# A hybrid decoder step on one core: attention units with a lag of three, exponentials between copies, and cached pages in two groups

## What is computed

```
s = einsum('bhmqk', q, k) * ATTN_SCALE           # two maps m, causal mask
p = softmax(s)                                   # per map
attn = p[map 0] - lam * p[map 1]
o = attn @ v ; o = o * rsqrt(mean(o^2) + eps) * g * (1 - lam_init)
```

## Time and profile before

| what | value |
|---|---|
| median of three runs | 4176.69 us |
| the profiled execution, its own time | 4166.23 us |
| its span | 4164.5 us |
| mean granted TensorE clock | 0.896 |
| PE, DVE, ACT, POOL busy over the span | 84%, 46%, 32%, 38% |
| attention phase in the span (first load to the next phase's first load) | 2593.1 to 3205.8 us |
| first and last row maximum (units 0 and 63) | start at 2618.43 and 3181.89 us |
| row maximum of unit 28, of unit 43 | start at 2889.82 and 3011.80 us |

### The profile page before, as it was taken

The page is one execution under the profiler, slowest core; times in us unless marked ns, Lnnn a source line. Parts: engine busy times, 40 slices in busy tenths (PEclk is TensorE's granted clock), DMA queues, the critical chain, the costliest instruction groups (busy, mean ns, idle before and its releaser), DMA issues. The chain is left out here.

```text
span 4164.5 us, 78261 instructions
## 1 busy us (share of the span) xinstructions
PE 3483.6 (84%) x34038; PEld 3147.2 (76%) x34038; DVE 1899.8 (46%) x2159; ACT 1346.4 (32%) x2059; POOL 1563.1 (38%) x648
## 2 busy tenths in 40 slices
PE   5889686898897298999999999455775989999896
PEld 2888435888786188999999998333443889999896
DVE  3333606455542586353454430677433772522622
ACT  1111113433432134333333433333444333333332
POOL 0111000000000155656656665455000656556563
PEclk8999858999998599999999999667887999999998
DMA  5222123334331543445444665545353534444442
GB/s 191 83 85 73 46 92 126 122 113 149 114 105 48 167 124 115 133 131 152 141 138 140 183 188 158 193 152 202 137 202 102 163 104 139 127 138 140 125 141 71
DMA packets 710476, 546.83 MB, mean 131 GB/s; under 512 B 34763, under 2 KB 667491, under 8 KB 709885
## 3 DMA queue, kind: packets, MB, share of 16 engines
q1 hardware_dynamic: 664182, 473.18, 36.9%
q10 hardware_dynamic: 45606, 67.55, 4.7%
q0 software_dynamic: 352, 1.18, 0.1%
HBM read 471.55 MB, written 70.29 MB: 130 GB/s over the span
## 5 line engine op out<-in xcount | busy, mean ns | idle before, releaser
L1630 POOL TENSOR_TENSOR dense_w_lo<-dense_w_raw,dense_w_hi 128x1024 fp32r<-128x1024 f32 x504 | 1273.4, 2532 | 974.8 <-ACT dense_w_hi L1701 974.6
L1686 PE MATMUL acc<-dense_x_hi,dense_w_hi 128*128 128x344 f32 x2496 | 813.2, 330 | 86.2 <-DVE dense_x_lo L1791 41.4
L1687 PE MATMUL acc<-dense_x_lo,dense_w_hi 128*128 128x344 f32 x2496 | 802.3, 326 | 0.0
L1701 ACT ACTIVATE dense_w_hi<-dense_w_raw 128x1024 fp32r<-128x1024 f32 x504 | 531.1, 1056 | 628.8 <-PE acc L1691 536.0
L1686 PEld LDWEIGHTS acc<-dense_x_hi,dense_w_hi 128*128 128x128 f32 x2496 | 482.4, 193 | 98.6 <-issue 79.7
L1687 PEld LDWEIGHTS acc<-dense_x_lo,dense_w_hi 128*128 128x128 f32 x2496 | 482.6, 193 | 2.5 <-issue 0.9
L1686 PE MATMUL acc<-dense_hid_hi,dense_w_hi 128*128 128x344 f32 x1536 | 483.4, 319 | 0.5 <-DVE dense_hid_lo L1811 0.5
L1687 PE MATMUL acc<-dense_hid_lo,dense_w_hi 128*128 128x344 f32 x1536 | 483.4, 319 | 0.0
L1691 PE MATMUL acc<-dense_x_hi,dense_w_lo 128*128 128x344 f32 x2496 | 449.7, 323 | 1.3 <-POOL dense_w_lo L1630 1.3
L1691 PEld LDWEIGHTS acc<-dense_x_hi,dense_w_lo 128*128 128x128 f32 x2496 | 409.9, 190 | 2.1 <-POOL dense_w_lo L1630 1.8
L750 POOL TENSOR_TENSOR x0T<-nT,levels 128x512 f32<-128x512 f32 x16 | 29.7, 1855 | 744.0 <-DVE bR L1249 744.0
(11 more groups left out here) (384 smaller groups left out, 5983.6 us busy)
## 6 DMA issues: line engine op xcount, KB each, us to landing
dense_w_raw<-in_ffn_w SPq DMA_DIRECT2D x384, 512.0 KB, 4.1
ada_quarter<-in_ada_w SPq DMA_DIRECT2D x40, 1024.0 KB, 11.0
att_k_page<-in_cache_k SPq DMA_DIRECT2D x64, 512.0 KB, 3.6
att_v_page<-in_cache_v SPq DMA_DIRECT2D x64, 512.0 KB, 5.9
scratch_mix<-proj_stage ACTq DMA_DIRECT2D x48, 516.0 KB, 2.7
scratch_mix<-dense_stage ACTq DMA_DIRECT2D x72, 172.0 KB, 2.1
w_raw<-in_a_w_rkv SPq DMA_DIRECT2D x24, 512.0 KB, 4.2
dense_w_raw<-in_a_w_o SPq DMA_DIRECT2D x24, 512.0 KB, 4.5
```

The costliest lines, as they stand in the source:

```text
L1630: nc.gpsimd.tensor_tensor(wlo[:, i % NW], raw[:, i % NRAW], whi[:, i % NW].bitcast(F32), ALU.subtract).then_inc(S("lo"), 1)
L1686: T_.matmul(out, whi[:, s % NW, k, :], a, start=j.first and k == 0, stop=False)
L1687: T_.matmul(out, whi[:, s % NW, k, :], b, start=False, stop=False)
L1701: A(whi[:, i % NW], raw[:, i % NRAW], ACT.Copy).then_inc(S("hi"), 1)
```

## The change

What it does:

- The lag goes from two units to three (`LAG`): PE in unit u turns and multiplies the probabilities of unit u - 3. The combined buffers `at` are doubled to four, and the small per-unit columns (maxima, sums, ratio) go from two sets to four.
- ACT makes the exponentials of unit u - 1 in unit u, one map after each of the unit's two copies, in place of those of unit u after `take`.
- On PE `values` is split in two parts, and one extra round stands between the turn of round 1 and part 1.
- The ratio is a TENSOR_SCALAR with two per-partition scalars in place of a SCALAR_TENSOR_TENSOR.
- The 64 K pages are taken 1.5 per unit over units 0 to 42 (`pages_of`: one page in even units, two in odd), in a product ring of three.
- The samples stand in two groups of four (`GS`), each with its own turn of scores, softmax and turn back (64 rows in place of 128), at units 22 and 43 (`SM`); the samples' V products stand at units 28, 32, 36, 40, 49, 52, 55, 58 (`VU`). V pages are loaded one per unit from unit 16; the reload of the ring follows one unit after each V product.
- At the start mask, k and q are loaded first, scores(0) stands ahead of the samples' rounds, and the samples' q, k and v are turned in three steps with a semaphore count each.
- `osq`, `ss` and the head scaling stand one unit later each (3, 4, 5 after a head).

Constants, buffers and the plan of the pages:

```diff
-        KU = NPAGE // 2
-        SM, V0, VSTEP = KU, KU + 6, 3
-        END = NU + 10
+        GS, GR = NS // 2, NS // 2 * 16
+        SM, VU = (22, 43), (28, 32, 36, 40, 49, 52, 55, 58)
+        END, LAG = NU + 10, 3
...
-        at = (sb("attn_long", [P, SEQ]), sb("attn_short", [P, SEQ // 2]))
+        at = (sb("attn_long", [P, 2, SEQ]), sb("attn_short", [P, 2, SEQ // 2]))
...
+        def pages_of(u):
+
+            return range(min(NPAGE, 3 * u // 2), min(NPAGE, 3 * (u + 1) // 2))
```

SyncE and GpSimd:

```diff
-                for j in (2 * u + NK, 2 * u + NK + 1):
-                    if j < NPAGE:
-                        k_page(j)
-                        if j % NP == NP - 2 and 1 < j // NP + 1 < NS:
-                            q_row(j // NP + 1)
+                for j in pages_of(u):
+                    if j + NK < NPAGE:
+                        k_page(j + NK)
+                    if j % NP == NP - 2 and 1 < j // NP + 1 < NS:
+                        q_row(j // NP + 1)
...
-                b = sample_of(u)
+                b = sample_of(u - 1)
                 if b is not None:
                     while vj < NPAGE and (vj - NV) // NP <= b:
                         v_page(vj)
...
-                        need(pool, "red", j - 1)
...
+                    need(pool, "red", j - NR + 1)
```

TensorE:

```diff
             for u in range(END):
-                w = u - 2
+                w = u - LAG
                 live = 0 <= w < NU
                 if live:
                     need(pe, "attn", w + 1)
-                    turn4(("attn", w, 0), [at[kind(w)][:, j * P:j * P + P] for j in range(min(4, blocks(w)))])
-                if u < NU:
+                    turn4(("attn", w, 0), [attn_of(w)[:, j * P:j * P + P] for j in range(min(4, blocks(w)))])
+                if 0 < u < NU:
                     scores(u)
+                todo = extras(u)
                 if live and blocks(w) > 4:
-                    turn4(("attn", w, 1), [at[kind(w)][:, j * P:j * P + P] for j in range(4, blocks(w))])
-                for name in extras(u):
+                    turn4(("attn", w, 1), [attn_of(w)[:, j * P:j * P + P] for j in range(4, blocks(w))])
+                    values(w, 0)
+                elif live and todo:
+                    extra(todo.pop(0))
+                    values(w, 0)
+                elif live:
+                    values(w, 0)
+                if live and blocks(w) > 4:
+                    if todo:
+                        extra(todo.pop(0))
+                    values(w, 1)
+                for name in todo:
                     extra(name)
-                if live:
-                    values(w)
```

VectorE:

```diff
-                need(dve, "take", u - 1)
+                need(dve, "take", u - 3)
...
-                V.scalar_tensor_tensor(w1[:, kd, 0:1], rl[:, kd, 1:2], lam[:, 0:1], l[:, kd, 0:1], ALU.mult, ALU.mult).then_inc(S("ratio"), 1)
+                V.tensor_scalar(w1[:, c, 0:1], rl[:, c, 1:2], l[:, c, 0:1], lam[:, 0:1], ALU.mult, ALU.mult).then_inc(S("ratio"), 1)
...
                 if u < NU:
                     maxima(u)
-                if u < KU:
-                    page_sums(2 * u)
+                todo = list(pages_of(u))
+                if todo:
+                    page_sums(todo.pop(0))
                 if 1 <= u <= NU:
                     combine(u - 1)
-                if u < KU:
-                    page_sums(2 * u + 1)
+                for j in todo:
+                    page_sums(j)
```

ScalarE:

```diff
             for u in range(END):
-                w = u - 2
-                for name in attn_rounds(w):
-                    turned(name)
+                w = u - LAG
+                for i in range(2):
+                    for name in attn_rounds(w)[i:i + 1]:
+                        turned(name)
+                    if 1 <= u <= NU:
+                        exps(u - 1, (i,))
                 for name in extras(u):
                     extra(name)
                 if 0 <= w < NU:
                     take(w)
-                if u < NU:
-                    exps(u)
```

More of the change, by code:

```diff
@@ L1964, in extras @@
                 out.append(("fin", h - 1, r - 6))
[L1965 to L1969, removed]
+            g = group(u, 0)
+            if g is not None:
+                out += [("page_sc", g, 0), ("page_sc", g, 1), ("page_new", g, 0)]
+            g = group(u, 3)
+            if g is not None:
+                out += [("page_back", g, 0), ("page_back", g, 1), ("new_back", g, 0)]
+            if u == SM[1] + 7:
                 out.append(("new_all", 0, 0))
@@ L1984, in attention_phase @@
         nth = {}
-        for name in [("rows", 0, i) for i in range(4)] + [n for u in range(END) for n in attn_rounds(u - 2) + extras(u)]:
+        for name in [("rows", 0, i) for i in range(4)] + [n for u in range(END) for n in attn_rounds(u - LAG) + extras(u)]:
             nth[name] = len(nth)
@@ L2111, in scores, with values @@
                 last.then_inc(S("s_mm"), 1)
-            def values(w):
+            def values(w, part):
                 h, n = w // KC, blocks(w)
[L2115 to L2119, removed]
+                if part == 0:
+                    need(pe, "take", w)
+                    need(pe, "t_in", nth["rows", h, 3] + 1)
+                need(pe, "t_in", nth["attn", w, part] + 1)
+                for j in range(4 * part, min(n, 4 * part + 4)):
                     last = T_.matmul(ob[:, 0:P], aT[kind(w)][:, j * P:(j + 1) * P], vrow[:, h % 2, j, :],
                                      start=(j == 0), stop=(j == n - 1))
-                last.then_inc(S("o_mm"), 1)
+                if j == n - 1:
+                    last.then_inc(S("o_mm"), 1)
             def extra(name):
@@ L2166, in extra, with sample_turn @@
                 last.then_inc(S("t_mm"), 1)
[L2168 to L2173 removed]
+            def sample_turn(t, banks):
+                for h in range(NH):
+                    last = T_.transpose(banks[0:NS, h // 4, (h % 4) * P:(h % 4 + 1) * P], t[:, h, :], m.ident[:])
+                last.then_inc(S("qkv_t"), 1)
+            need(pe, "consts", 2)
+            need(pe, "in_k", 16)
+            scores(0)
+            pe.wait_ge(S("cols_in"), 48)
+            sample_turn(qs, six[:, 4:6, :])
+            sample_turn(ks, m.aux2)
+            need(pe, "sample_rows", 1)
+            sample_turn(vs, six[:, 4:6, :])
+            need(pe, "sample_rows", 2)
             need(pe, "consts", 4)
@@ L2286, in _ @@
[L2286 to L2292 removed]
+                g = group(u, 1)
@@ L2317, in _ @@
             A(ls[:], ls[:], ACT.Exp).then_inc(S("lam_exp"), 1)
-            need(act, "qkv_t", 1)
-            for i in range(3):
-                A(rows[:, i, :].rearrange("p (a n) -> p a n", a=2), (m.acc[0], m.acc[1], m.aux2)[i][0:NS, 0:2, :],
-                  ACT.Copy).then_inc(S("sample_rows"), 1)
+            for i, banks in enumerate((six[:, 4:6, :], m.aux2, six[:, 4:6, :])):
+                need(act, "qkv_t", i + 1)
+                A(rows[:, i, :].rearrange("p (a n) -> p a n", a=2), banks[0:NS], ACT.Copy).then_inc(S("sample_rows"), 1)
             def head_rows(h, part):
```

170 lines of the change are left out of this document (91 added, 79 removed).

## The result

The changed kernel took 4033.88 us, median of four runs (4022.81 to 4039.25), against 4173.39 for the kernel before in the same company: a ratio of 0.9664 [0.9637, 0.9691], 140 us less. The prediction said 4079, with 4040 to 4127. The number is that of rival 1 (4035), and the profile must say whether its mechanism is too.

The account below looks back on a forecast made before the run. A PE-DVE chain was taken to bound units 0 to 27, PE the later ones; 75 + 5 + 20 + 1.5 - 3 = 98.5 us off 4166.23 gives 4068, plus 10.5 to the median: 4079 us, range 4040 to 4127.

Parts of the forecast that it names:

- rival 1: Products find other places, DVE is freed of holds, first stretch falls to PE's 153 us: total 4035 us, chance 0.08.
- Units 0 to 27: First stretch: DVE bounds at 190 us plus 6 for head scalings behind products, 7.0 a unit; gain 75 us.
- The loop and its cure: Units 0 to 27: PE and DVE work adds up, 118.0 us of PE waits on combinations; lag of three cuts it.
- The ratio: DVE's one-element ratio in its new form: credited nothing, bounds nothing to 42 us.
- The trade: On DVE, when the ratio passes a POOL product, the combination behind it is held in its place.
- The doubt over TENSOR_SCALAR: Not sure this form escapes the hold: the negated maximum, one too, took 1.03 us beside a product.
- Units 28 to 42: Middle stretch: PE bounds at 115 to 117 us, with four V products at 8.8 each, above DVE's 105; gain 5.
- Units 43 to 63: Last stretch: two samples leave (17.6 us), six rounds come (6), 8 of PE's 34.9 idle saved; gain 20.
- a rising clock as a sign: Units 0 to 27: clock above 0.68 expected because PE works more densely there; no gain priced.
- Ends: Phase's start: new load order gains 1.5 us; phase's end: one more unit to turn loses 3.
- Rival 2: Combinations wait for exponentials now a unit later on ACT, 2 us in each unit: 4135 us, chance 0.10.
- Rival 3: V page reloads on SP at units 29, 33, 37, 41 starve K pages, stopping DVE: 4198 us, chance 0.03.

Follow-up runs that it names:

- lag2: The changed kernel with the lag set back from three units to two, all else kept: 4154.75 us, ratio 0.9969.
- lag_only: The kernel before with only the lag of three and its doubled combined buffers, all else as before: 4133.28 us, ratio 0.9908.
- pages2: The changed kernel with two K pages a unit again over units 0 to 31, as before the change: 4057.86 us, ratio 0.9715.
- sums_late: The changed kernel with all page sums of a unit behind the combination on DVE: 4021.47 us, ratio 0.9637.
- late_split: The changed kernel with page sums behind the combination and the negated maximum split into two one-element instructions: 4005.58 us, ratio 0.9597.
- both_old: The changed kernel with ACT's old order (exponentials after take) and PE's old order of rounds, all else kept: 4093.56 us, ratio 0.9808.

## Why the prediction was right, and where it was not

**Units 0 to 27 (gain 75, measured 73.6).** The loop and its cure were read rightly: `lag2` brings the waits on the combination back, `lag_only` removes them. DVE bounds: `pages2` lengthens the stretch by 36 us. The pace forecast was 7.0; it is 6.81 in units 1 to 27, and the 13.9 of unit 0 makes up the difference. But that the stretch hit its forecast is in part luck, since DVE's busy time was 177.8 and not 196. With the ratio in its old form it is 190.1 and 189.0: the 190 was right, the nothing for the ratio was wrong by 12, and the 6 for head scalings held behind a product did not come (two of them in this stretch, 1.22 us each in both kernels). Against these 18 us stand 20 of idle time that I had put at nothing: 10.3 for the first product, 4.4 for exponentials, 2.3 for scores and 3 in small gaps.

**The ratio (gain 0).** The trade was right: combinations held, not freed, so rival 1's mechanism did not happen and that its time did is a coincidence. But the trade isn't even; by the medians it returned some 5 us of the run. The doubt over TENSOR_SCALAR is resolved by form: of one element it was not held in 27 of 27 units (0.27 us, though a product ran beside 26 of them), of two it was (1.24 us on average in `sums_late`), and the same work split into single elements was not (0.154 and 0.144). The Trainium skill (VectorE: DVE Perf Modes, "Mode 2×_2P — use both read ports for one tensor") says that an instruction in this mode gives each read port one half of its data, and asks for an outermost non-unit dimension that is even, or odd and equal for source and destination. A single element has no such dimension, and what becomes of it the page doesn't say; in these rows it is not held as one that takes the second port would be.

**Units 28 to 42 (gain 5, measured 18.0).** I had PE bound this stretch, at 115 to 117 us, above DVE's 15 x 7.0 = 105. What stands there is DVE's 104.1: it is busy for 92.9 of them, and with DVE relieved the stretch falls to 97.0 (`pages2`), 96.3 and 95.5 (`sums_late`, `late_split`). So PE's sum was some 20 us too high, and the price of a V product is part of that. A V product was put at 8.8 us of PE with its waits. PE's two groups after, over the last two stretches:

```profile
L2173 PE MATMUL aux<-att_v_page,att_page_attn 128*32 128x512 f32 x232 | 28.0, 598 | 4.6 <-ACT att_page_o L2432 2.5 <-ACT att_v_rows L2374 0.9 <-ACT att_attn_cols_long L2395 0.9
...
L2180 PE MATMUL aux<-att_fold,att_page_o 128*128 128x1 f32 x128 | 15.5, 251 | 0.4 <-ACT att_attn_new_all L2430 0.3
```

With 32 of these matmuls to a product, the 232 are 7.25 products: 32.6 / 7.25 + 15.9 / 8 = 6.5 us each, 2.3 less than before. Four times that is 9; and 24 of the first product's 32 matmuls (3.4 us) now ran ahead of the maxima of unit 28. Together that is 12.6 us off PE's sum, enough to bring it down to DVE's; the rest of the 20 I did not trace. The cheaper part is again waits and shorter rows (598 ns against 654, and 251 against 283).

**Units 43 to 63 (gain 20, measured 41.0).** This is the step that failed. I took 8 us of PE's 34.9 idle and it was 10.0: right in size. I took the samples' two V products off PE's busy time, added the turning rounds, and carried every duration over from rows taken at a clock of 0.81. By those terms PE would be busy for 125.8 us (135.2 less the 13.4 of two products without their waits, plus about 4 of the rounds); it was 104.2. The 21 us missed here are thus work that ran faster, not idle time. I had named a rising clock as a sign in the first stretch and priced it at nothing anywhere. The orders give most of it: with both old the clock is 0.81 again, PE's busy time 120.6 and the stretch 161.0, so 16.4 of the 21.6 us come back. The other 5 do not; in `both_old` the scores of 512 columns take 711 ns where they took 870 before at the same mean clock, and 757 in the changed kernel at 0.92, so a stretch's mean clock does not give the time of one kind of matmul. Why the low clock falls on other instructions there was not tested.

**Ends (gain 1.5, loss 3).** The start gained 12.0 us by the first maximum, of which 10.3 came back as the wait for the first product, which leaves 1.7; the end lost nothing (23.9 to 23.1). **Rivals.** Rival 2's sign, the reciprocal waiting on exponentials, cost DVE 4.4 us in two units of the first stretch, not in each. Rival 3: SyncE waited 8.0 us, once, in the middle stretch, for a V product, and DVE did not starve. Neither happened.

Of the phase's 145.4 us, 98.5 were forecast. The rest is 9 at the start and in the first stretch, 13 in the middle, 21 in the last and 4 at the end.

## What to carry to other kernels

Where a change removes waits of PE between short matmuls, its other work can get cheaper too (here by 16 us of a stretch of 129); price PE's rows of before at the clock that the denser stretch will have, or give the range an end for it. An engine's hold by another is not removed by changing the instruction that it catches: look which instruction comes next, and whether that one can be caught; in the three edits that freed one here, half or more of what was freed came back (25 of 41 us, 19 of 32, 13 of 27). And an order of instructions on ACT that lets a copy for a single PSUM buffer pass ahead of long exponentials can be worth as much (38 us here, with the lag of three in place) as the deeper pipeline alone (36 to 38).

## What the runs showed of the hardware

A DVE TENSOR_SCALAR of one element a partition is not held by a GpSimd product beside it (0.27, 0.154 and 0.144 us), while one of two elements is (1.24 us on average, up to 2.33). A held combination ends 0.28 us behind the product that held it, where one that starts only then ends 0.53 behind it: 2.66 us in place of 2.91 for the pair. And nearly the same idle time of PE in one stretch went with clocks of 0.83, 0.91 and 0.86 (29.2, 29.9 and 30.5 us; one profile each).
